# HGRN heads of a hybrid encoder layer: score products inserted three times a head, with one level in the other bank

## What is computed

```python
def hgrn_step(s_state, inp):
    q, k, v, lf = inp
    causal = jnp.tril(jnp.ones((length, length), dtype=bool))[:, :, None]
    a = jnp.cumsum(lf, axis=2)
    rel = jnp.where(causal, a[:, :, :, None, :] - a[:, :, None, :, :], -jnp.inf)
    scores = jnp.einsum('bhtk,bhsk,bhtsk->bhts', q, k, jnp.exp(rel))
    o = jnp.einsum('bhtk,bhkv->bhtv', q * jnp.exp(a), s_state) + jnp.einsum('bhts,bhsv->bhtv', scores, v)
    a_end = a[:, :, -1:]
    s_new = jnp.exp(a_end[:, :, 0])[..., None] * s_state + jnp.einsum('bhsk,bhsv->bhkv', k * jnp.exp(a_end - a), v)
    return s_new, o
```

## Time and profile before

| | |
|---|---|
| median of three runs | 2222.31 us |
| profiled execution | 2221.52 us, its span 2219.7 us |
| TensorE (PE) busy | 2186.7 us, 99% |
| VectorE (DVE) busy | 1347.9 us, 61% |
| ScalarE (ACT) busy | 788.0 us, 36% |
| L1497, pair products, 560 records in four heads | 19.8 us |
| granted clock of TensorE, mean | 0.998 |

### The profile page before, as it was taken

The page is one execution under the profiler, slowest core; times in us unless marked ns, Lnnn a source line. Parts: engine busy times, 40 slices in busy tenths (PEclk is TensorE's granted clock), DMA queues, the critical chain, the costliest instruction groups (busy, mean ns, idle before and its releaser), DMA issues.

```text
span 2219.7 us, 44655 instructions
## 1 busy us (share of the span) xinstructions
PE 2186.7 (99%) x18901; PEld 2151.0 (97%) x18901; DVE 1347.9 (61%) x2105; ACT 788.0 (36%) x1209; POOL 63.8 (3%) x93
## 2 busy tenths in 40 slices
PE   6999999999999999999999999999999999999997
PEld 5999999999999999999999999999999999999997
DVE  5444444488777777676657484755777755454354
ACT  5321221234333333333334242424333443244443
POOL 0000001000000000000000000000000000000000
PEclk9999999999999999999999999999999999999999
DMA  5422222233333333334112121204111353434465
GB/s 184 134 79 97 84 86 90 76 106 119 121 135 110 120 120 124 126 119 169 59 52 83 42 74 45 88 22 151 67 67 67 112 207 139 163 138 171 151 216 181
DMA packets 67352, 249.33 MB, mean 112 GB/s; under 512 B 9082, under 2 KB 16428, under 8 KB 50612
## 3 DMA queue, kind: packets, MB, share of 16 engines
q1 hardware_dynamic: 67204, 247.14, 32.1%
HBM read 216.92 MB, written 30.19 MB: 111 GB/s over the span
## 4 chain that ended last, share of the span: by engine, by line
PE 98%; DMA 1%; DVE 0%; SPq 0%; ACT 0%; issue 0%; DVEq 0%; POOL 0%; ACTq 0%; POOLq 0%
PE acc L1009 52%; PE acc L1198 16%; PE branch L1198 8%; PE acc L1608 7%; PE branch L1608 2%; PE branch L1297 1%; PE branch L1497 1%; PE branch L1313 1%; PE branch L1322 1%; DMA scratch<-in_x_all 1%; PE acc L1052 1%; PE branch L1287 0%; PE branch L1365 0%; PE branch L1628 0%; PE branch L1144 0%; PE branch L1137 0%
## 5 line engine op out<-in xcount | busy, mean ns | idle before, releaser
L1009 PE MATMUL acc<-act_hi,w_hi 128*128 128x320 f32 (+3 forms) x2848 | 869.0, 305 | 0.0
L1009 PE MATMUL acc<-act_lo,w_hi 128*128 128x320 f32 (+3 forms) x2848 | 845.4, 297 | 0.0
L1009 PE MATMUL acc<-act_hi,w_lo 128*128 128x320 f32 (+3 forms) x2848 | 845.4, 297 | 0.0
L1009 PEld LDWEIGHTS acc<-act_hi,w_hi 128*128 128x128 f32 x2848 | 537.3, 189 | 11.0 <-issue 5.0
L1009 PEld LDWEIGHTS acc<-act_lo,w_hi 128*128 128x128 f32 x2848 | 537.2, 189 | 0.7
L1009 PEld LDWEIGHTS acc<-act_hi,w_lo 128*128 128x128 f32 x2848 | 537.0, 189 | 0.0
L2149 DVE TENSOR_TENSOR w_lo<-w_raw,w_hi 128x2048 fp32r<-128x2048 f32 x119 | 272.5, 2290 | 228.1 <-ACT w_hi L1666 225.6
L1666 ACT ACTIVATE w_hi<-w_raw 128x2048 fp32r<-128x2048 f32 x120 | 229.8, 1915 | 132.9 <-PE branch L1608 125.7
L1198 PE MATMUL acc<-corner_terms,w_hi 128*128 128x288 f32 x768 | 154.5, 296 | 0.0
L1198 PE MATMUL acc<-act_hi,w_hi 128*128 128x288 f32 x512 | 151.6, 296 | 0.0
L1198 PE MATMUL acc<-act_lo,w_hi 128*128 128x288 f32 x512 | 151.4, 296 | 0.0
(11 more groups left out here) (470 smaller groups left out, 3502.9 us busy)
## 6 DMA issues: line engine op xcount, KB each, us to landing
w_raw<-in_w_stream SPq DMA_DIRECT2D x122, 1024.0 KB, 4.8
w_raw<-in_w_stream SPq DMA_DIRECT2D x96, 512.0 KB, 5.9
gate_logits<-gate_out SPq DMA_DIRECT2D x48, 288.0 KB, 2.2
scratch<-gate_logits SPq DMA_DIRECT2D x48, 288.0 KB, 5.2
scratch<-in_x_all SPq DMA_DIRECT2D x9, 512.0 KB, 6.0
branch_rows<-branch_out SPq DMA_DIRECT2D x16, 288.0 KB, 2.2
scratch<-in_x_all SPq DMA_DIRECT2D x3, 1024.0 KB, 10.7
out_y_prompt<-scratch SPq DMA_DIRECT2D x6, 512.0 KB, 3.0
```

Of the source, the lines that this page charges most:

```text
L1009: last = mm(acc[s][:, at:at + hi - lo], a[:, s, w], b[:, k, lo:hi], start=(k == order[0] and a is whi and b is xh), stop=(k == order[-1] a ...
```

## The change

The plan has three inserts of pairs instead of four: the same-token pairs with levels 0 and 1 at block 12; levels 2, 3 and 4 at block 24; levels 5 and 6 at block 32, as before. The keys are turned at block 16 instead of 14, and the values at 28, apart from the pairs, instead of behind those of block 26. A table says where each level's scores lie; levels 1 and 4, third of their inserts, use `bra` at column 0. So `turn_k` now waits for masked1, and `turn_v` for masked4. VectorE's order is changed to match: masked1 follows masked0, and masked2 stands ahead of masked3, behind the arguments of level 6. ScalarE's order stays.

```diff
     "hgrn_vector": """
         logit logit0 soft_inv softmax bound rest f1 f2 f3 f k log_copy log_sums end_args args0 scaled0 args1
-        ends khat meta_from_zero scaled1 args2 scaled2 args3 masked7 masked0 scaled3 args4 masked1 masked2
-        scaled4 args5 scaled5 args6 masked3 masked4 scaled6 masked5 masked6 state1 state2 state3 state4
+        ends khat meta_from_zero scaled1 args2 scaled2 args3 masked7 masked0 masked1 scaled3 args4
+        scaled4 args5 scaled5 args6 masked2 masked3 masked4 scaled6 masked5 masked6 state1 state2 state3 state4
         states z1 z2 gate o_unit y""",
...
-        pairs7 pairs0 k_turned pairs1 pairs2 pairs3 pairs4 v_turned pairs5 pairs6 updates outputs
+        pairs7 pairs0 pairs1 k_turned pairs2 pairs3 pairs4 v_turned pairs5 pairs6 updates outputs
         o_turned""",
...
+        scores_at = [(brb, 512), (bra, 0), (brb, 0), (brb, 512), (bra, 0), (brb, 0), (brb, 512), (brb, 0)]
...
-                    qk, o = QK[lv % 4], 512 * ((lv + 1) % 2)
+                    qk, (bank, o) = QK[lv % 4], scores_at[lv]
...
-                def two_levels(lv):
-                    if lv < 0:
-                        same_token()
-                    else:
-                        pe.wait_ge(*vt.after(i, "masked0" if lv == 1 else f"scaled{lv + 1}"))
+                def first_levels():
+                    same_token()
+                    level_pairs(0)
+                    level_pairs(1)
+
+                def middle_levels():
+                    pe.wait_ge(*at.after(i, "k_rows"))
+                    pe.wait_ge(*vt.after(i, "scaled4"))
+                    for lv in (2, 3, 4):
                         level_pairs(lv)
-                    level_pairs(lv + 1)
+
+                def last_levels():
+                    pe.wait_ge(*vt.after(i, "scaled6"))
+                    level_pairs(5)
+                    level_pairs(6)
...
                 def turn_k():
-                    pe.wait_ge(*vt.after(i, "khat"))
+                    pe.wait_ge(*vt.after(i, "masked1"))
                     turn_rows(khat, bra, "k_turned")
 
                 def turn_v():
                     pe.wait_ge(evac_done, N(2) + 1)
-                    pe.wait_ge(*at.after(i, "k_rows"))
+                    pe.wait_ge(*vt.after(i, "masked4"))
                     turn_rows(bv, bra, "v_turned")
...
-                plan = ([(14, turn_k)] + [(block, lambda lv=lv: two_levels(lv)) for lv, block in ((-1, 11), (1, 17), (3, 26), (5, 32))]
-                        + [(26, turn_v), (32, updates), (38, outputs), (47, turn_o)])
+                plan = [(12, first_levels), (16, turn_k), (24, middle_levels), (28, turn_v), (32, last_levels), (32, updates),
+                        (38, outputs), (47, turn_o)]
...
                 same_token()
                 level_masked(0)
+                level_masked(1)
                 level_scaled(3)
                 level_args(4)
-                level_masked(1)
-                level_masked(2)
                 level_scaled(4)
                 level_args(5)
                 split_lo(N(4))
                 level_scaled(5)
                 level_args(6)
+                level_masked(2)
                 level_masked(3)
                 level_masked(4)
                 level_scaled(6)
```

More of the change, by code:

```diff
@@ L1491, in hgrn_head, with half_pairs @@
                 sides = [slice(0, 64), slice(64, 128)]
-                def half_pairs(k, q, o):
+                def half_pairs(k, q, bank, o):
                     for c in range(NCH):
@@ L1496, in half_pairs @@
                             tok = slice(START[c] + 64 * h, START[c] + 64 * h + 64)
-                            last = mm(brb[r, o + 64 * c:o + 64 * c + 64], k[:, tok], q[:, tok], start=True, stop=True)
+                            last = mm(bank[r, o + 64 * c:o + 64 * c + 64], k[:, tok], q[:, tok], start=True, stop=True)
                     return last
@@ L1502, in level_pairs @@
                     pe.sem_inc(pairs_begun, 1)
-                    qk, o = QK[lv % 4], 512 * ((lv + 1) % 2)
+                    qk, (bank, o) = QK[lv % 4], scores_at[lv]
                     if lv < LEVELS - 1:
-                        last = half_pairs(qk, qk, o)
+                        last = half_pairs(qk, qk, bank, o)
                     else:
                         for c in range(1, NCH):
-                            last = mm(brb[0:64, o + 64 * c:o + 64 * c + 64], qk[:, START[c]:START[c] + 64], qk[:, START[c] + 64:START[c] + P], start=True, stop=True)
+                            last = mm(bank[0:64, o + 64 * c:o + 64 * c + 64], qk[:, START[c]:START[c] + 64], qk[:, START[c] + 64:START[c] + P], start=True, stop=True)
                     pt.done(last, f"pairs{lv}")
@@ L1514, in same_token @@
                     pe.sem_inc(pairs_begun, 1)
-                    pt.done(half_pairs(bk, bq, 0), f"pairs{LEVELS}")
-                def two_levels(lv):
-                    if lv < 0:
-                        same_token()
-                    else:
-                        pe.wait_ge(*vt.after(i, "masked0" if lv == 1 else f"scaled{lv + 1}"))
+                    pt.done(half_pairs(bk, bq, *scores_at[LEVELS]), f"pairs{LEVELS}")
+                def first_levels():
[6 more added lines that the diff above has]
+                    for lv in (2, 3, 4):
                         level_pairs(lv)
-                    level_pairs(lv + 1)
+                def last_levels():
+                    pe.wait_ge(*vt.after(i, "scaled6"))
+                    level_pairs(5)
+                    level_pairs(6)
                 def updates():
@@ L2826, in level_masked @@
                     dve.sem_inc(masks_begun, 1)
-                    o = 512 * ((lv + 1) % 2)
-                    bank = brb[:, o:o + 5 * 64].rearrange("p (c n) -> p c n", c=5)
+                    psum, o = scores_at[lv]
+                    bank = psum[:, o:o + 5 * 64].rearrange("p (c n) -> p c n", c=5)
                     V.done(v.copy_predicated(PSD[:, :, :], chosen(lv).bitcast(mybir.dt.uint16).to_broadcast([P, NCH, 64]), bank), f"masked{lv}")
```

## The result

The changed kernel takes 2228.85 us (median of 8 runs, 2228.22 to 2229.7) against 2222.31 for the kernel before (2221.72 to 2223.25): 6.5 us more, ratio 1.0031 with a 95% interval of 1.0022 to 1.0040. The forecast was 2227.8 in a range of 2225.2 to 2229.6. The profiled execution took 2228.39 us, span 2226.6, which is 6.9 over the span before. The prediction put the spread of the kernel before at 0.25 us, from three runs; in these eight it is 1.5 us.

A forecast was written before the change was run, and what follows sets the result against it. TensorE, busy 98% of the span, was taken to bound the kernel. Heads 2 to 4 add 3.3 us and the first 2.35, 5.65, taken as 5.5: 2227.8 against the median of 2222.31, range 2225.2 to 2229.6.

The forecast's parts named there:

- The values' turn: At block 28 of each head: TensorE waits 1.00 us for masked4 and restarts for 0.1, 1.1 us a head.
- T: Start of the keys' turn in a head, from which the prediction counts the times of later steps.
- the chain: From the keys' turn over ScalarE's exp3 and exp4 and VectorE's scaled4 to args6, then masked2 to masked4, ending at T + 13.18.
- the restart: TensorE starting again after a wait on VectorE: an estimate of 0.1 us added to each wait.
- The keys' turn: At block 16: waits for masked1, 0.15 us in heads 2 to 4; in the first head 1.3 plus 0.1 restart.
- the hole in VectorE: First head, between scaled1's two operations: 1.19 us without a dependency, expected again; rival that it stays away: 2226.5, 27%.
- the one of 1.3 us that I named as a sign: First head, keys' turn: a TensorE wait of 1.3 us expected in the changed kernel's profile, under 0.3 in the others.
- The saving: TensorE's inserts in each head: 5.60 us before, 5.45 after, 0.15 us saved a head, 0.6 in all.
- The sum over the heads: Heads 2 to 4 add 3.3 us, the first head 2.35: 5.65, taken as 5.5.
- a further hole of VectorE: Rival: a hole like the first head's on the chain in another head, +1.2 us, 2229.0; chance 12%.
- no wait at all: Rival: masked4 reaches TensorE before T + 12.24, only the saving remains, 2221.7; chance 7%.
- The granted clock: Rival: waits of 1 us bring TensorE's clock to 1.2 GHz, +3.2 us a head, 2240; chance 2%.

The follow-up runs named there:

- blocks 29 and 30: Two runs: values turned at block 29, or at block 30, instead of 28, against the changed kernel: 2225.80 us and 2227.56 us.
- early masks: Changed kernel with VectorE's masks of levels 2 to 4 ahead of scaled5 and args6 instead of behind them: 2224.24 us.
- exp4: Changed kernel with ScalarE's exp4 ahead of the split of the next tile's weights instead of behind it: 2227.04 us.
- the kernel in which the waits are really gone: Changed kernel with masks 2 to 4 ahead of scaled5, inserts at 13, 18, 26, 29 (first head) and 12, 17, 25, 29, 397 wait instructions: 2221.52 us.

## Why the prediction was right, and what it missed

- **The values' turn** was the deciding term, forecast at 1.1 us a head with the turn at T + 13.24. It came at T + 13.30 after a listed wait of 0.95. Moving TensorE's question (blocks 29 and 30), VectorE's order (early masks) and ScalarE's order (exp4) each moved the wait by the amount that the chain gives, so this cause is shown. From the matmul ahead of it the turn stands 1.25 us (1635.57 to 1636.82), where 0.13 is usual: 1.12 us for the wait and the restart, against 1.1. It starts 0.15 behind the end of the last mask copy (1636.67), where the forecast had 0.06 and 0.1.
- **The keys' turn** was given 0.15 us in heads 2 to 4; it cost 0.19. In the first head it was 1.4 with the hole in VectorE, which I expected to recur: it did, and the head as a whole grew by 2.37 against 2.35 forecast. But the wait was not the one of 1.3 us that I named as a sign. I had checked the third level of the insert against scaled1 only in the second head; in the first the hole delays scaled1 too, and 0.33 us of the wait were paid there and 0.78 at the turn.
- **The saving** of 0.15 us a head was right in sign and small in size: 0.2 where it can be seen alone.
- **The sum over the heads** was 5.65, measured 5.6. I took 5.5 of it, as the restarts might overlap the latency; they didn't.
- **What failed** is a sentence of the first part: "whatever TensorE loses or saves in the four heads reaches the end undiminished". It did, but I took the stretch behind the heads to be the same in both kernels. It is 1.3 us longer, a term that the sum has at nothing. The change moved TensorE's code by four wait instructions, and the adding and removing of four shows that this sets the hole. I counted matmuls in the order of instructions and not the waits that they can't carry. The hole is a pause of 1.24 us of TensorE's sequencer on entering a loop, with nothing in the dependencies behind it. That it fetches code there is the likely reading, and it is not shown: the instruction packets that the DMA trace has around this place, one of 16 KiB and one of 8, stand at the same matmuls in the kernels with and without the hole.
- **Luck.** The measured 2228.85 is 1.05 above the forecast and lies in the range, but the 1.3 us that took it there are not what the range was opened for: larger waits, and a further hole of VectorE on the chain between T and masked4. The waits came out as forecast and no such hole came; a hole of like size came elsewhere, for a reason that the prediction doesn't have. Without it the kernel would have stood near 2227.6, 0.2 from the forecast.
- **The rivals**: no wait at all would have been 2221.7, and the kernel in which the waits are really gone comes to 2221.5. Beside that kernel the one before took 2222.08, though, and the two are not to be told apart. A further hole on VectorE's chain didn't appear. The granted clock stayed at 1.00 through waits of 0.95 us in every head (1600 to 1663.5) and through the hole in the output product (1800 to 2190), so a wait of this length is no case for the prediction's warning against any new idle time.

## What to carry to other kernels

Where one engine is busy all the time, an insert that is moved earlier or later is safe only if the chain that feeds it is: write down when its last operand is ready, counted from the last step of the bound engine on which that chain hangs, and compare it with when the engine will ask. Merging inserts saved 0.2 us a head, and one wait added to free a bank cost five times that. When waits are added to an engine's program, look for new idle time far behind the change as well, since code that nobody touched has moved: here it was at the entry of a loop, some 330 us behind the last head.

## What the runs showed of the hardware that I had not expected

- Four more wait instructions in TensorE's program bring a hole of 0.9 us at one matmul, the first of a loop some 370 us behind the last of them, in all seven kernels that have them, and none in the three that don't. The sequencer's records show the pause between two of its own instructions, 1.23 to 1.24 us against 0.06.
- VectorE's hole in the first head is at the same instruction in all ten kernels, with 1.16 to 1.42 us (1.19 in the kernel before, 1.24 in the changed one). So it isn't an accident of one run, and in the kernel before it was invisible in the time.
- A wait of TensorE on VectorE of 0.19 us isn't listed by the profile: the matmul ahead is recorded with 0.29 us and the turn starts 0.32 behind its start. Only distances from start to start show it.
